# A hybrid encoder layer on eight cores: decay of past keys taken relative to a block's first query, weight loads in quarters, value groups between key, query and gate groups

## What is computed

```python
cum = jnp.transpose(jnp.cumsum(logf, axis=1), (0, 2, 1))            # logf = log_sigmoid(x w_f + b_f)
s = jnp.einsum('bqhd,bkhd->bhqk', qi, k).astype(jnp.float32) * scale
s = s + ci[..., :, None] - cum[:, :, None, :]
s = jnp.where(k_pos[None, :] <= pi[:, None], s, NEG_INF)
p = jax.nn.softmax(s, axis=-1).astype(v.dtype)
o = jnp.einsum('bhqk,bkhd->bqhd', p, v)                             # then o * silu(gate)
```

## Time and profile before

| | |
|---|---|
| median of 3 runs | 3450.51 us (3449.12 to 3451.85) |
| the profiled execution's own time | 3459.89 us |
| its span on the slowest core (core 4) | 3458.3 us |
| spans of the 8 cores | 3434.4 to 3458.3 us |
| PE busy | 3329.8 us (96%), 18998 matmuls |
| DVE, ACT, POOL busy | 1198.0, 915.5, 860.8 us |
| chain of work that ended last | PE 88%, DMA 4%, issue 2%, DVE 2%, ACT 2%, POOL 1% |

### The profile page before, as it was taken

The page is one execution under the profiler, slowest core; times in us unless marked ns, Lnnn a source line. Parts: engine busy times, 40 slices in busy tenths (PEclk is TensorE's granted clock), DMA queues, the critical chain, the costliest instruction groups (busy, mean ns, idle before and its releaser), DMA issues.

```text
span 3458.3 us, 54793 instructions; the slowest of 8 cores (3434.4 to 3458.3 us)
## 1 busy us (share of the span) xinstructions
PE 3329.8 (96%) x18998; PEld 1643.9 (48%) x18998; DVE 1198.0 (35%) x1989; ACT 915.5 (26%) x1571; POOL 860.8 (25%) x1045
## 2 busy tenths in 40 slices
PE   7899999999998999999999999999999999999997
PEld 4555555555544444444444444455544444444443
DVE  0476666667676222222211111111112232111465
ACT  1355555455554111111111111111113331111111
POOL 2233333333334222222200000222221113322233
PEclk9999999999999999999999999999999999999999
DMA  9634333433331313131224443866662115665643
GB/s 166 122 74 81 73 81 70 81 70 71 73 66 33 49 25 49 25 49 25 46 58 104 109 92 81 167 152 141 154 144 48 25 25 126 137 144 140 206 151 118
DMA packets 151702, 315.80 MB, mean 91 GB/s; under 512 B 32112, under 2 KB 57328, under 8 KB 146940
## 3 DMA queue, kind: packets, MB, share of 16 engines
q0 software_dynamic: 39232, 134.54, 24.5%
q1 hardware_dynamic: 112200, 177.76, 17.0%
HBM read 351.46 MB, written 95.32 MB: 129 GB/s over the span
## 4 chain that ended last, share of the span: by engine, by line
PE 88%; DMA 4%; issue 2%; DVE 2%; ACT 2%; POOL 1%; POOLq 0%; ACTq 0%; DVEq 0%; SPq 0%
PE bank L146 88%; DMA m_scr<-mt 1%; DMA xT<-xTp 1%; DMA fv_p<-v 1%; ACT ge L163 1%; DVE st L181 1%; DVE acc L173 1%; POOL aC L173 0%; ACT pt L163 0%; POOL pt L169 0%; DMA wcb<-wcM 0%; ACT k L168 0%; ACT rl L163 0%; POOL mt L173 0%; POOL pt L705 0%
## 5 line engine op out<-in xcount | busy, mean ns | idle before, releaser
L146 PE MATMUL bank<-xT,wcb 128*128 128x512 bf16 (+1 forms) x3840 | 728.2, 343 | 7.1 <-DMA wcb<-wcM 6.5
L146 PE MATMUL bank<-xT,cwb 128*128 128x512 bf16 (+1 forms) x3840 | 702.5, 343 | 8.9 <-DVE us L173 8.1
L146 PE MATMUL bank<-xT,wkqg 128*128 128x512 bf16 (+1 forms) x2880 | 608.3, 348 | 8.7 <-DMA wkqg<-wkqg 5.0
L146 PEld LDWEIGHTS bank<-xT,wcb 128*128 128x128 bf16 x3840 | 327.1, 98 | 370.3 <-issue 13.5
L146 PEld LDWEIGHTS bank<-xT,cwb 128*128 128x128 bf16 x3840 | 325.1, 98 | 373.4 <-issue 16.4
L173 DVE TENSOR_TENSOR mt<-bank,gt 128x512 f32<-128x512 f32 (+1 forms) x240 | 143.5, 598 | 1032.5 <-PE bank L146 883.5
L163 ACT ACTIVATE pt<-st,ncc 128x512 bf16<-128x512 f32 (+4 forms) x492 | 314.8, 647 | 427.0 <-DVE st L181 352.0
L163 ACT ACTIVATE gt<-bank,bm 128x512 f32<-128x512 f32 (+1 forms) x240 | 147.0, 612 | 969.0 <-PE bank L146 965.0
L146 PEld LDWEIGHTS bank<-xT,wkqg 128*128 128x128 bf16 x2880 | 245.4, 99 | 274.1 <-issue 35.2
L181 DVE SCALAR_TENSOR_TENSOR st<-bank,cq 128x512 f32<-128x512 f32 x480 | 291.3, 608 | 201.0 <-PE bank L146 172.9
L173 DVE TENSOR_TENSOR acc<-acc,pt 128x512 f32<-128x512 f32 (+3 forms) x396 | 260.7, 658 | 0.9 <-POOL pt L705 0.4
(11 more groups left out here) (137 smaller groups left out, 2543.8 us busy)
## 6 DMA issues: line engine op xcount, KB each, us to landing
m_scr<-mt SPq DMA_DIRECT2D x128, 256.0 KB, 2.2
pv<-m_scr SPq DMA_DIRECT2D x128, 256.0 KB, 5.5
cwb<-wc POOLq DMA_DIRECT2D x12, 2048.0 KB, 16.8
wkqg<-wkqg POOLq DMA_DIRECT2D x11, 1536.0 KB, 15.1
mw<-wm POOLq DMA_DIRECT2D x16, 1024.0 KB, 13.9
x<-xp SPq DMA_DIRECT2D x16, 1024.0 KB, 7.2
y_p<-rr SPq DMA_DIRECT2D x16, 1024.0 KB, 4.8
wcb<-wcC POOLq DMA_DIRECT2D x16, 896.0 KB, 10.8
```

The lines of the kernel that those rows point to most:

```text
L146: return lambda e: e.matmul(out, lhsT=lhsT, rhs=rhs, start=start, stop=stop)
```

## The change

Below the diagonal the decay is no longer added per query. ACT exponentiates straight from the score bank, with the scale and a bias per key that holds the key's decay relative to the block's first query (`nb`, made by POOL a head ahead). The rest, a decay per query (`fq`, made by ACT), is multiplied in once per block: into the sums when the last tile below the diagonal is in, and into the output, for which the parts below and on the diagonal have banks of their own. Diagonal tiles go the old way. The sample's cached keys are treated likewise, with eight exponentials of 64 columns, since each key chunk has its own bias.

The order of blocks becomes 0, sample, 1, 3, 2 (in head 0: 0, 1, sample, 3, 2), scores run LA = 4 tiles ahead, and there are nine `pt` buffers and two `st`. The steps at a block's end move: DVE makes `hi`, `lo` follows one tile later, and the logarithm, the exponential and the finish are separate steps. In attention the gate's logarithm and last exponential are put off by one and two tiles. The fill list deals the value groups out, two before each key, gate or query group, and ends with the sample's, block 3's and block 2's query and gate groups (block 2's not before tile 35). Weight loads are cut in four and issued at set tiles from `hooks`. In the prologue one query group moves ahead of the transposes of the forget logits, the first value weights lie in rows of 288 columns (268 used), and a mask that was no longer read is not loaded. In the convolution the sample's four groups follow one each behind blocks 0 to 3, with buffers of their own. The last token chunk is normalised in quarters, two by ACT and POOL and two by DVE, with a DMA each.

```diff
-    wvf = [bw("wv0", [128, 16 * 268], BF16, r_vw[0]), bw("wv1", [128, 16 * 256], BF16, r_vw[1])]
+    wvf = [bw("wv0", [128, 16 * 288], BF16, r_vw[0]), bw("wv1", [128, 16 * 256], BF16, r_vw[1])]
...
-    run_all(k_group(0, 3))
+    run_all(k_group(0, 3) + q_group(0, 3))
...
-    NST, NPT = 3, 7
+    NST, NPT = 2, 9
...
+        dg = lambda tb: [(h, tb, kc) for kc in range(4 * tb, 4 * tb + 4)]
+        of = lambda tb: [(h, tb, kc) for kc in range(4 * tb)]
+        one, late = of(1) + dg(1), [(h, 4, 0), (h, 4, 1)]
+        tiles += dg(0) + (one + late if h == 0 else late + one) + of(3) + dg(3) + of(2) + dg(2)
...
+    def make_bias(h, tb):
...
+        S.add(POOL, TS(nb[p][:, c0:c0 + n], ncc[:, k0:k0 + n, h:h + 1].rearrange("p a b -> p (a b)"), ref, ALU.add),
+              reads=[rr, r_ncc], writes=[r_nb[p][tb]])
+        c = 4 * p + tb - 1
+        S.add(POOL, TS(nr[:, c:c + 1], ref, -1.0, ALU.mult), reads=[rr], writes=[r_nr[p][tb]])
...
+            if diag:
...
+            else:
+                c = NB0[tb] + kc
+                S.add(ACT, ACTF(pt[p][:], banks[sb_][:], AF.Exp, bias=nb[h % 2][:, c:c + 1], scale=SCALE),
+                      reads=[bankr[sb_], r_nb[h % 2][tb]], writes=[r_pt[p]])
...
+            for c in range(8):
+                S.add(ACT, ACTF(pt[p][:, c * NS:(c + 1) * NS], banks[sb_][:, c * NS:(c + 1) * NS], AF.Exp,
+                                bias=nb[h % 2][:, 24 + c:25 + c], scale=SCALE),
+                      reads=[bankr[sb_], r_nb[h % 2][4]], writes=[r_pt[p]])
...
+    def make_decay(h, tb):
...
+        S.add(ACT, ACTF(out[:], src, AF.Exp, bias=nr[:, c:c + 1]), reads=[rs, r_nr[h % 2][tb]], writes=[ro])
...
+    def next_decays(i, h, tb):
+        if h + 1 < H:
+            load_cq(h + 1, tb)
+            later.append((i + 8, lambda: make_bias(h + 1, tb)))
...
+            if kc == 4 * tb - 2:
...
+                make_decay(h, tb)
+            if kc == 4 * tb - 1:
+                S.add(DVE, TT(A[:], A[:], fq[:], ALU.mult), reads=[rA, r_fq], writes=[rA])
             if last:
                 hi, lo = take_pt((i, 0)), take_pt((i, 1))
-                S.add(POOL, COPY(pt[hi][:], A[:]), reads=[rA], writes=[r_pt[hi]])
+                S.add(DVE, COPY(pt[hi][:], A[:]), reads=[rA], writes=[r_pt[hi]])
...
+                    S.add(DVE, TT(fq[:], banks[Of][:], fq[:], ALU.mult), reads=[bankr[Of], r_fq], writes=[r_fq])
+                    S.add(DVE, TT(fq[:], banks[Ob][:], fq[:], ALU.add), reads=[bankr[Ob], r_fq], writes=[r_fq])
+                    finish_block(h, tb, rl[:], r_rl, fq[:], [r_fq], 512)
-                later.append((i + 2, s1))
+                later.append((i + 1, s1))
                 later.append((i + 3, s2))
-                later.append((i + 6, lambda: finish_block(h, tb, rl[:], banks[Ob][:], Ob, 512)))
+                later.append((i + 4, s2b))
+                later.append((i + 6, s3))
...
-    LA = 3
+    LA = 4
...
+            nv = (len(vs) // 4 + len(rest) - 1) // len(rest)
+            for grp in rest:
+                fill += vs[:4 * nv] + grp
+                vs = vs[4 * nv:]
+            fill += q_group(n, 4) + g_group(n, 4)
+            for tb in (3, 2):
+                fill += q_group(n, tb, past_block[tb]) + g_group(n, tb, past_block[tb])
...
+        for q in range(4):
             if h + 2 < H:
-                load_kw(h + 2)
-            if h % 2 == 0 and h // 2 + 2 < 6:
-                load_vw(h // 2 + 2)
+                hooks.setdefault(12 + 6 * q, []).append(lambda q=q: load_kw(h + 2, q, q + 1))
+            if h % 2 == 1 and h // 2 + 2 < 6:
+                hooks.setdefault(9 + 6 * q, []).append(lambda q=q: load_vw(h // 2 + 2, q, q + 1))
...
+            gs = [group(cmm(1, tb), tn, ev_c), group(cmm(2, tb), tn, ev_h), group(cmm(0, tb), tn, ev_b), group(cmm(3, tb), tn, ev_g)]
+            if tb == 4:
+                late = gs
+            else:
+                out += gs[0] + gs[1] + gs[2] + gs[3] + late[tb]
...
+            center(0)
...
+            scale(POOL, 0)
+            center(1)
+            scale(POOL, 1)
+            center(2)
+            scale(DVE, 2)
+            center(3)
+            scale(DVE, 3)
```

More of the change, by code:

```diff
@@ L463, in build @@
     pj = [0]
+    held = set()
     def nextbank():
-        b = (0, 1, 7)[pj[0] % 3]
-        pj[0] += 1
-        return b
+        while True:
+            b = (0, 1, 7)[pj[0] % 3]
+            pj[0] += 1
+            if b not in held:
+                return b
     def group(mm, ncols, evict, n=16, step=4, need=-1):
@@ L484, in build @@
     k32i, v32i, gei = [0], [0], [0]
+    now = [None]
+    later = []
     d_fl = S.dmasem("fl")
@@ L824, in issue_PV, with s3 @@
+            make_decay(h, 4)
             if h + 1 < H:
                 load_cache(h + 1)
-                load_cq(h + 1, 4)
+        else:
+            Ob = obank[(h, 4)]
+            vv, rv = vslice(h, 16, NS)
+            S.add(PE, MM(banks[Ob][:, 2 * NS:3 * NS], vv, pt[p][0:NS, 0:NS], True, True), reads=[r_pt[p], rv], writes=[bankr[Ob]])
+            S.add(PE, MM(banks[Ob][:, 3 * NS:4 * NS], onesb[0:NS, :], pt[p][0:NS, 0:NS], True, True),
+                  reads=[r_pt[p], r_const], writes=[bankr[Ob]])
+            for out, ro, k in ((os_, r_os, 0), (fs, r_fs, 1)):
+                S.add(DVE, TT(out[:], banks[Ob][:, k * NS:(k + 1) * NS], fs[:], ALU.mult), reads=[bankr[Ob], r_fs], writes=[ro])
+                S.add(DVE, TT(out[:], banks[Ob][:, (k + 2) * NS:(k + 3) * NS], out[:], ALU.add), reads=[bankr[Ob], ro], writes=[ro])
+            held.discard(Ob)
+            row_recip(fs[:], r_fs, fs[:], r_fs)
+            def s3():
+                finish_block(h, 4, os_[:], r_os, fs[:], [r_fs], NS)
+            later.append((i + 2, s3))
+            next_decays(i, h, 4)
@@ L828, in colsof @@
     def colsof(i):
-        h, tb, kc, first, last = tiles[i]
+        h, tb, kc = tiles[i]
         if tb == 4:
@@ L844, in main_pieces @@
                 out.append((colsof(i + LA), lambda i=i: issue_S(i + LA), -1))
-            if tiles[i][1] == 1 and tiles[i][2] == 3:
-                out.append((0, lambda: make_csd(h), -1))
             out.append((colsof(i) + PAD, lambda i=i: issue_PV(i), i))
+            out += [(0, fn, -1) for fn in hooks.get(i - first_of[h], ())]
         return out
@@ L946, in conv_pieces @@
-            out += group(cmm(1, tb), tn, ev_c)
-            out += group(cmm(2, tb), tn, ev_h)
-            out += group(cmm(0, tb), tn, ev_b)
-            out += group(cmm(3, tb), tn, ev_g)
+                    S.add(ACT, ACTF(sc[:, 0:tn], sc[:, 0:tn], AF.Ln, bias=1.0), reads=[rsc], writes=[rsc])
+                    S.add(ACT, ACTF(sc[:, 0:tn], sc[:, 0:tn], AF.Exp, scale=-1.0), reads=[rsc], writes=[rsc])
+                    S.add(POOL, TT(sc[:, 0:tn], sc[:, 0:tn], sx[:, 0:tn], ALU.mult), reads=[rsc, r_sx], writes=[rsc])
@@ L1005, in build @@
         fn()
+    later[:] = []
+    now[0] = None
     M.free("qT0", "qT1", "qT2", "qT4", "sg0", "sg1", "sg2", "sg4", "qs0", "qs1", "sgs0", "sgs1", "cq", "cqs0", "cqs1", "kT1", "vb1", "kcT", "vc",
[L1009 removed]
+           *[f"st{i}" for i in range(NST)], *[f"pt{i}" for i in range(NPT)], "rl", "fq", "acc0", "acc1", "ao0", "ao1", "nr0", "os")
     O_AC = O_A
```

329 lines of the change are left out of this document (191 added, 138 removed).

## The result

| | before | after |
|---|---|---|
| median of the runs | 3451.18 us (4 runs, 3449.12 to 3452.45) | 3412.4 us (3412.28, 3412.52) |
| ratio after / before | | 0.9888, 95% interval 0.9864 to 0.9912 |
| span of the slowest core | 3458.3 us (core 4) | 3410.7 us (core 7) |

The change is worth 38.8 us, 1.1%; the prediction said 68, with a range that holds the result. All times here are of undisturbed executions, except that one die of the profiled execution of *eight unchained* (3424.3 us) ran at a lower clock than the other, so that cores 0 to 3, on the undisturbed die, are read of it.

A forecast was written before the change was run, and what follows sets the result against it. TensorE was taken as busy nearly throughout, so gains come from idle time and half-clock stretches. Attention -52, convolution -8.5, before attention -3.5, start +1, tail -5 give -68: 3382.5 us, range 3345 to 3425.

The forecast's parts named there:

- The seam: Between two heads in attention: TensorE's waits fall from 2.6 to 1.4 us, -13 over 11 seams; clock drops behind, -6.
- the hidden part: Attention: some 45 of 71 waits go, each worth 0.17 us more than its row shows, -7.5 us.
- the seam is as long as before: Rival, chance 0.20: between heads, waits, clock drops and their hidden part, 23 us, stay; 3405.5 us.
- Value groups and loads: Attention: value groups alternating with others and loads in four pieces end DVE's holds for value outputs, -10.5 us.
- Sums inside a head: Blocks ending mid-head: with the sums' bf16 copy on DVE, TensorE's waits for POOL's copy and DVE's remainder go, -7 us.
- end of attention: Last block's sum: the 4.9 us wait for POOL's copy falls to 1.5, -3.4, and -1.5 for a clock drop.
- Convolution: At channel tile ends: TensorE's ten waits for the sample's product, 8.1 us, and remaining idle go, -8.5 us.
- Before attention: Prologue: a query group fills TensorE's 3.5 us wait for the forget logits, -3.5 us.
- Start: First loads: the first value weights, no longer packed, become 2048 packets instead of 512, +1 us.
- Tail: After the last sum: normalising the last chunk in quarters on DVE, ACT and POOL, -5 us.
- ACT holds the score banks: Slower rival, chance 0.08: gate and key-copy bursts on ACT keep score banks longer than TensorE has fill, +18, 3468.5 us.
- Bias columns and output banks: Attention: POOL's bias waiting for decay rows and ACT's decay vector for joined banks cost 0 to +1 a head, taken as 0.

The follow-up runs named there:

- eight unchained: The changed kernel with the sample's eight exponentials no longer waiting on semaphores for one another: 3398.7 us, median of three runs.
- the wide pass: The changed kernel with one 512-column DVE instruction and one 512-column exponential for the sample's cached keys instead of eight small exponentials: 3392.2 us.
- the reversal: The changed kernel with four edits outside attention undone (convolution's sample groups, first value weights, prologue query group, last chunk's normalisation): 3433.9 us.

## Why the prediction was right, and where it was not

**The direction and the range were right, the size was not**, and nearly all of the difference lies in attention. Part of this is luck. The 3412.4 us lie outside the 3355 to 3403 that the forecast had by itself, in a range that was drawn wider for its rivals. And what the sum set at nothing, the fourth tile ahead and the split itself, made good some of what its terms did not bring.

By kind, the step that failed is the waits: -35.4 us of them were to go in attention and 8.5 went, while the clock, given -9, brought -15.5.

*The seam* was to go from 2.6 to 1.4 us, with "0.5 for the eight small exponentials ahead in the queue". That term was mis-sized. The price of one was at hand, and eight of them were counted in ACT's sum (2.75 us), but on the path only 0.5 of it. In the seam too little lies beside them, and the whole 3.15 us, with 1.74 ahead in which ACT is not yet free, stands between the scores and the release of their bank. (The 2.6 left out 0.31 for DVE's remainder; with it that seam has 2.9.) The waits came out at 2.9 us, as before, and the hidden part stayed with them. With the eight replaced or moved attention is 20.5 to 20.8 us shorter, -45 against before: then the prediction's total is nearly reached, and the wide pass's seams wait 1.5 us in the mean, about its 1.4. The drop of the clock went even so, further than the half that was taken (-6): it came behind eight of these seams before and comes behind one now on most cores. So *the seam is as long as before*, at 0.20 the likeliest of the rivals, had the waits right and "the clock still drops" wrong, and its 3405.5 us lie near the measured time in part by chance. Of its reasons "ACT has more to do there" was the cause; "fill is still held to tile 5" was at most a small part, since fill put ahead of it took 0.7 us from a seam and was missed behind it.

*Value groups and loads* (-10.5) measured 1.6 and 2.0, no more than two executions of one program differ. DVE's holds did go, by the quarters, but with them back TensorE lost hardly anything, since the split had taken its off-diagonal scores off DVE. The gain was put to the wrong edit: the split itself had been set at 0.

*Sums inside a head* (-7) and *end of attention* (-4.9): 4 to 6 together. The last block's wait of 4.9 us became one of 4.4 for DVE; 1.5 had been left for it. DVE is late there with the sums themselves, of which passes next to POOL's work take 1.44 and 1.50 us where 0.69 is usual, and with two copies for the convolution.

*What the sum did not have* is the fourth tile ahead, named under the seam and given no price: 13.2 us when it is undone alone, at the two ends of attention above all. The rest of the gain, 2.4 us a head, belongs to the split, order, gates and the smaller moves that no run took apart.

*Convolution* (-8.5): -12.2, and the reversal gives 11.4. The direction and cause were right; the 0.17 us hidden in each wait, 1.7 for ten of them, was counted in attention and not here, and the last 1 to 2 us stay open. *Before attention* (-3.5): -3.1, and 4.1 by reversal; the cover that the scans lost shows no cost beside the 4 us by which the cores differ in this stage. *Start* (+1): +1.5, and 0.8 by reversal, but the eleven other kernels here that have this prologue need 35.8 to 36.5 us, which makes it up to +3. The first queue of the first 52 us (packets, MB, share; compare) moved 3% fewer bytes in 1484 more packets:

```profile
q0 software_dynamic: 3834, 7.11, 92.3%
```

A MB then took 6% more of the engines' time, 2.6 us over the 16 of them, an estimate from these two rows. So the price lies between the bytes (0) and the packets (+4.2), and the term was rather too small. *Tail* (-5): -3.1, with two DVE passes that took twice as long beside POOL's additions.

*The signs* named beforehand fall the same way. Right: no wait for POOL's copy, none for the sample's product, none of DVE for value outputs, the convolution at 632 us. Wrong: attention at 957 instead of 930, and DVE's scores still at 18.0 us, now from the diagonal tiles and the last heads. A clock near 0.71 behind the seams, named as a sign against, is there on the slowest core in three of eleven and is the exception on most. TensorE's 26.8 us of the first 52 stayed above the 26.5 that would have spoken against the start.

*ACT holds the score banks*, the slower rival, had the mechanism and the wrong place: not the gates in mid-head, where fill covers them, but the sample's burst in the seam. *Bias columns and output banks* at 0 held: no such wait is in the list but one of 1.3 us for `fq`.

## What to carry to other kernels

Price a burst not by its share of an engine but by how long it holds the buffer the next step needs, at the place where it stands: the same 3.15 us cost 1.81 of waiting in a thin seam and 0.18 in mid-head. When one instruction is cut into several, look at what the scheduler books as written, because dependences inside one engine can undo the overlap. Before adding up the gains of several edits, ask which of them removes the reason for another. And read waits and clock apart, on all cores: the slowest core showed a drop behind a seam that six of the eight did not have.

## What the runs showed of the hardware

Small exponentials that wait for one another by semaphore took 0.39 us each, the same instructions without these waits 0.22. DVE passes of 0.74 us took 1.50 and 1.74 beside POOL's additions. And the length of the waits in a seam does not settle the clock behind it: behind 0.46 and some 1.8 us of waiting at the same place of the same program the next five us had 0.66 on core 7 and 1.00 on core 0, and behind the wide pass's seam, TensorE busy for 4.43 of 5 us, 1.00.
